# A two-block transformer kernel on one core: order of scores, exponentials and copies in its attention loops, and where the modulation matrix is multiplied

## The reference

```
first layer, differential attention (4 heads, two maps m = 0, 1 of width 64 each):
    p = softmax(q_m k_m^T / 8 - slope * |i - j|);  out = (p_0 - lam p_1) v
first layer, sparse attention (4 heads of width 64):
    of the allowed keys only the 256 with the highest index score count, the others get -inf
    out = softmax(q k^T / 8 - slope * |i - j|) v
second layer, forgetting attention (8 heads of width 64):
    cum_f = cumsum(log_sigmoid(f));  logits = q k^T / 8 + cum_f[q] - cum_f[k]  (causal)
second layer, modulation:
    mod = silu(c) @ w_ada + b_ada          (w_ada is 1024 x 6144, 24 MB)
```

## Time and profile before

| | |
|---|---|
| median of three runs | 3118.78 us |
| the profiled execution | 3110.41 us, span of its instructions 3108.7 us |
| TensorE busy | 2970.8 us, 96% |
| VectorE, ScalarE, GpSimd busy | 1343.3, 632.2, 1390.0 us |
| mean granted TensorE clock | 0.985 |
| loop of `diff` | about 434 to 559 us from the start |
| loop of `sparse` | about 559 to 655 us |
| loop of `forget` | about 1731 to 1886 us |

### The profile page before, as it was taken

The page is one execution under the profiler, slowest core; times in us unless marked ns, Lnnn a source line. Parts: engine busy times, 40 slices in busy tenths (PEclk is TensorE's granted clock), DMA queues, the critical chain, the costliest instruction groups (busy, mean ns, idle before and its releaser), DMA issues.

```text
span 3108.7 us, 33231 instructions
## 1 busy us (share of the span) xinstructions
PE 2970.8 (96%) x13501; PEld 2204.0 (71%) x13509; DVE 1343.3 (43%) x2012; ACT 632.2 (20%) x1056; POOL 1390.0 (45%) x814
## 2 busy tenths in 40 slices
PE   7999989889999999999999898999998999999997
PEld 4544446567888888888788556667667888887886
DVE  0499957646532324433514653111313433234323
ACT  1411036431110001111211462001112211111111
POOL 2000000035666566666677003444446666666663
PEclk8999999999999999999999999999999999999999
DMA  4111124532333333333433001332333233333331
GB/s 99 35 34 41 34 75 110 137 137 88 95 102 102 95 97 100 116 101 95 122 89 101 14 1 51 91 119 71 82 103 121 88 102 89 102 94 122 94 103 62
DMA packets 364919, 273.22 MB, mean 88 GB/s; under 512 B 14048, under 2 KB 334816, under 8 KB 364768
## 3 DMA queue, kind: packets, MB, share of 16 engines
q1 hardware_dynamic: 357568, 253.30, 28.4%
q10 hardware_dynamic: 4720, 10.68, 0.9%
q0 software_dynamic: 2480, 7.13, 0.7%
HBM read 262.59 MB, written 8.49 MB: 87 GB/s over the span
## 4 chain that ended last, share of the span: by engine, by line
PE 87%; DVE 4%; DMA 3%; issue 2%; POOL 2%; ACT 1%; SPq 0%; DVEq 0%; POOLq 0%; ACTq 0%
PE PS L809 39%; PE PS L821 24%; PE PS L761 5%; PE PS L775 4%; DMA ring<-in_w_in 3%; PE PS L446 2%; PE PS L1013 2%; PE PS L881 2%; PE PS L464 2%; PE PS L484 2%; POOL w_low L1883 1%; PE PS L476 1%; PE PS L895 1%; PE PS L738 1%; DVE arena L550 1%
## 5 line engine op out<-in xcount | busy, mean ns | idle before, releaser
L1883 POOL TENSOR_TENSOR w_low<-ring,w_high 128x1024 fp32r<-128x1024 f32 x382 | 938.1, 2456 | 31.8
L1880 POOL TENSOR_SCALAR w_high<-ring 128x1024 fp32r<-128x1024 f32 x382 | 425.7, 1114 | 1019.6 <-PE PS L821 371.6
L821 PE MATMUL PS<-w_high,hid_high 128*128 128x512 f32 x864 | 336.4, 389 | 9.1 <-issue 9.1
L821 PE MATMUL PS<-w_high,hid_low 128*128 128x512 f32 x864 | 336.2, 389 | 0.0
L821 PE MATMUL PS<-w_low,hid_high 128*128 128x512 f32 x864 | 336.1, 389 | 0.0
L809 PE MATMUL PS<-hT_high,w_high 128*128 128x512 f32 x656 | 271.6, 414 | 12.6 <-POOL w_low L1883 12.6
L809 PE MATMUL PS<-x1T_high,w_high 128*128 128x512 f32 x704 | 274.9, 390 | 3.6 <-DVE x1T_low L1574 3.6
L809 PE MATMUL PS<-x1T_low,w_high 128*128 128x512 f32 x704 | 274.6, 390 | 0.0
L809 PE MATMUL PS<-x1T_high,w_low 128*128 128x512 f32 x704 | 274.5, 390 | 0.0
L809 PE MATMUL PS<-hT_high,w_low 128*128 128x512 f32 x656 | 256.3, 391 | 0.0
L809 PE MATMUL PS<-hT_low,w_high 128*128 128x512 f32 x656 | 256.2, 391 | 0.0
(11 more groups left out here) (268 smaller groups left out, 4623.9 us busy)
## 6 DMA issues: line engine op xcount, KB each, us to landing
ring<-in_w_ff SPq DMA_DIRECT2D x128, 512.0 KB, 3.8
ring<-in_w_in SPq DMA_DIRECT2D x112, 512.0 KB, 3.9
ring<-in_w_gu SPq DMA_DIRECT2D x88, 512.0 KB, 3.9
ring<-in_w_ada SPq DMA_DIRECT2D x48, 512.0 KB, 5.2
ring<-in_w_down SPq DMA_DIRECT2D x44, 512.0 KB, 3.6
ring<-in_w_out SPq DMA_DIRECT2D x32, 512.0 KB, 4.2
ring<-in_w_branch SPq DMA_DIRECT2D x16, 512.0 KB, 3.9
arena<-in_x SPq DMA_DIRECT2D x8, 512.0 KB, 7.5
```

The costliest lines, as they stand in the source:

```text
L821: mm = pe.matmul(PS[:, 2 * p + half, :], x[:, k, at], w[:, q, half_of(half)], start=(first and n == 0), stop=(last and n == 2))
L1880: pool.tensor_scalar(w_high[:, q, :], ring[:, s, :], 1.0, 1.0, ALU.mult, ALU.mult).then_inc(weights_high, 1)
L1883: pool.tensor_tensor(w_low[:, q, :], ring[:, s, :], w_high[:, q, :].bitcast(F32), ALU.subtract).then_inc(weights_used[s], 1)
```

## The change

In a chunk of scores the added product of a map now follows that map's own scores: scores 0, added 0, scores 1, added 1. In ScalarE's step, `exps(u+1)` now stands before `copy_turned(u-1)`. Of the 12 groups of `ada`, `diff` now takes ten (two units in three, instead of six groups in two units of five) and `sparse` two (instead of six in every unit's fill). Before the loop of `forget`, `copy_v2(1)` now stands before the wait for `cum_done` and the copies to `cum_r`.

```diff
@@ scores(u), TensorE
-                        more = [None if self.more is None else self.more(pe, u, m, c, w) for m in range(2)]
                         for m in range(2):
                             if c == 0 and u >= 1:
                                 pe.wait_ge(self.logits_made, 2 * u - 1 + m)
+                            more = self.more(pe, u, m, c, w) if self.more is not None else None
                             mm = pe.matmul(PS[:, 2 * m + c // 512, 0:w], self.q(j, m, b), self.k(j, m, c, w),
-                                           start=True, stop=more[m] is None)
-                            if c + w == N and more[m] is None:
+                                           start=True, stop=more is None)
+                            if more is not None:
+                                mm = pe.matmul(PS[:, 2 * m + c // 512, 0:w], *more, start=False, stop=True)
+                            if c + w == N:
                                 mm.then_inc(self.scores_done, 1)
-                        for m in range(2):
-                            if more[m] is not None:
-                                mm = pe.matmul(PS[:, 2 * m + c // 512, 0:w], *more[m], start=False, stop=True)
-                                if c + w == N:
-                                    mm.then_inc(self.scores_done, 1)
@@ the loop of act(), ScalarE
                 for u in range(last + 2):
+                    if u < last:
+                        exps(u + 1)
                     if u >= 1:
                         copy_turned(u - 1)
-                    if u < last:
-                        exps(u + 1)
@@ ada_fill
-        def ada_fill(first, groups, every):
+        def ada_fill(first, groups):
             def fill(pe, u):
-                if u % every < 2 and u // every < groups:
+                if u % 3 < 2 and u // 3 < groups:
                     for j in range(2):
-                        ada(pe, 4 * (first + u // every) + 2 * (u % every) + j)
+                        ada(pe, 4 * (first + u // 3) + 2 * (u % 3) + j)
             def after(act, u):
-                if u % every == 1 and u // every < groups:
-                    rows_out(act, first + u // every)
+                if u % 3 == 1 and u // 3 < groups:
+                    rows_out(act, first + u // 3)
-        fill_c, rows_c = ada_fill(6, 6, 2)
+        fill_c, rows_c = ada_fill(10, 2)
@@ diff
-            prob, probT, (4, 5), *ada_fill(0, 6, 5))
+            prob, probT, (4, 5), *ada_fill(0, 10))
@@ ScalarE before forget.act
             for u in range(1, 4):
                 copy_tiles("qk2", 1, u, qk2T)
+            copy_v2(1)
             act.wait_ge(cum_done, 1)
             for r in (slice(0, 8), slice(64, 72)):
                 act.copy(cum_r[r, :], fl[0:8, :]).then_inc(cum_high, 1)
-            copy_v2(1)
             forget.act(act)
```

## The result

The changed kernel takes 3198.90 us (median of four runs, 3195.68 to 3201.08), the kernel before on the same chip 3118.66 us. The ratio is 1.0263, with a 95% interval of 1.0244 to 1.0282: 80 us slower. The forecast was 3182 us with a range of 3150 to 3212.

A forecast was written before the change was run, and what follows sets the result against it. TensorE, busy 96% of the span, was taken to bound the kernel. `diff` 12, `sparse` 9 and `forget` 21.9 + 20 made 62.9 us on 3110.4: 3173.3, or 3182 at the median's level, range 3150 to 3212.

The forecast's parts named there:

- Part 1: Before `forget`: copies to `cum_r` behind `copy_v2` delay VectorE's whole queue and the first logits, +21.9 us.
- Part 2 in `forget`: ScalarE's copies, now behind the exponentials, make TensorE wait: 5.25 us a pass, taken as +20 us.
- The four places: In a `forget` pass, block 7 next +1.9, block 7 turned +1.0, block 5 next +0.6, block 5 turned +1.75 us.
- Part 2 in `diff`: Late copies delay `times_v`: 3.1 us a pass, 12.4 in four, of which 5 us kept because fills cover waits.
- Part 3: Added product between the maps' scores: 0 in `forget`, where maps still overlap; 15.7 us in `sparse`, where they run serially.
- Part 4: Fills of four `ada` groups move: +7.7 us in `diff`, -7.7 in `sparse`, which also loses three waits, -3.8.
- the nearly free part 2: Rival: early exponentials free VectorE and TensorE, and `sparse` idle time hides longer scores; 3148 us, chance 0.08.
- strict order: Rival: TensorE keeps matmuls in program order, so `forget` loses its map overlap too, +30 us; 3212 us, chance 0.13.
- the other side: Rival: exponentials in front end the three loops' idle time, up to -47.8 us against +21.9; 3093 us, chance 0.03.

The follow-up runs named there:

- part 1 alone: Kernel before with only `copy_v2(1)` moved ahead of the wait for `cum_done` and the copies to `cum_r`: 3135.50 us, ratio 1.0057.
- part 2 alone: Kernel before with only `exps(u+1)` put before `copy_turned(u-1)` in all three loops: 3160.46 us, ratio 1.0138.
- The added work: Whole change plus 16 unread float32 products in each of the twelve `sparse` units left without a fill: 3189.15 us, ratio 1.0233 against the kernel before.
- part 3 alone: Kernel before with only each map's added product put right behind its own scores: 3124.58 us, ratio 1.0020.
- any single part: Kernel before with one edit: `copy_v2` first 3135.50 us, exponentials first 3160.46, added product behind its scores 3124.58, `ada` groups ten and two 3108.23.
- pairs: Kernel before with two edits: score order and `ada` groups 3120.01 us; exponentials first and score order 3181.58; exponentials first and `ada` groups 3151.87.

## Why the prediction was right, and where its sum was off

The direction, the range and the order of size were right: 63 us forecast, 80 measured. Point by point:

- **Part 1, forecast +21.9, measured +18.** The mechanism is as described, instruction by instruction. The step "between 1711.25 and 1734.76 it has no hole that could take up a delay" was true and not enough: the stretch was stretched by GpSimd beside it, and 4 us of that vanished when it moved. The step "TensorE, with one unit of scores done" was wrong, since that unit waited as well (5.8 us with part 1 alone), but it changes nothing in the sum: the logits come last.
- **Part 2 in `forget`, forecast +20, measured +30.6.** The four places were real. With part 2 alone, in the pass of the earlier trace rows, the four together move TensorE by about 5 us where I had 5.25. The last three of them:

```profile
1815.60 1.06 PE L464 MATMUL PS<-ident,arena 128*128 128x128 f32 x8 [1.28 <-ACT arena L524]
1827.49 0.87 PE L484 MATMUL PS<-arena 128*64 128x256 f32 x8 [0.55 <-ACT arena L524]
1834.73 0.84 PE L464 MATMUL PS<-ident,arena 128*128 128x128 f32 x6 [2.18 <-ACT arena L524]
```

  In the earlier trace rows the same instructions waited 0.33, 0 and 0.55 us. After block 7 the change waits 1.69 us for the copies before `times_v`, where I had 1.9:

```profile
1844.09 3.18 PE L481 MATMUL PS<-arena 128*64 128x256 f32 x16 [1.69 <-ACT arena L521]
```

  That row also shows what the sum had left out: the same 16 instructions took 1.73 us before and 3.18 here, straight after the wait. The waits, 16.7 us more, are the term as forecast, a little smaller; the rest goes with 35 us more of low clock, which the sum had put at nothing.
- **Part 2 in `diff`.** Forecast 12.4 uncovered and 5 with the fills. Measured 13.4 alone, and 8.9 - 2.7 = 6.2 on top of the fills. Both numbers are near, and part of that is luck. The sum took only the new waits for copies, which grew by 11.7 us; 5.7 us of other waits went, so TensorE idled 5.9 us more, and lower clock made up the rest. Most of what the fills save is that clock, and 2 us of it are waits.
- **Part 3, forecast 0 in `forget` and 15.7 in `sparse`, measured 0 and 10.4.** The halves of the rows run side by side. In `sparse` they don't. Two of its chunks in a unit of block 7 after the change:

```profile
630.28 1.12 PE L446 MATMUL PS<-arena 64*128 64x512 f32 x2
631.65 1.12 PE L446 MATMUL PS<-arena 64*128 64x512 f32 x2 [0.25 <-issue]
632.71 0.39 PE L449 MATMUL PS<-arena 128*128 128x512 bf16 x1
633.03 1.12 PE L446 MATMUL PS<-arena 64*128 64x512 f32 x2
```

  Map 1 starts 1.37 us after map 0. From chunk to chunk it is 633.03 - 630.28 = 2.75 us, against 1.60 before:

```profile
608.47 1.13 PE L446 MATMUL PS<-arena 64*128 64x512 f32 x4
609.76 0.38 PE L452 MATMUL PS<-arena 128*128 128x512 bf16 x1 [0.16 <-issue]
610.07 1.13 PE L446 MATMUL PS<-arena 64*128 64x512 f32 x4
```

  So a chunk of 512 costs 1.15 us more, and the 1.13 was right. The idle time of 0.16 us before the mask, here and in the earlier trace rows, is none. The kernel has two mask products there, and the next chunk's row shows both (611.13, x2); in this one the profile holds only the second. In the rows after, the mask behind the first map is missing in the same way. A map's scores take 1.05 us from their start to the mask's, and the next scores start 0.32 us after the mask's, where one mask follows another in 0.23. That the loop paid 5 us less than forecast goes with 3.5 us less of idle time (15.9 to 12.4 us) and with a clock of 0.99 instead of 0.97.
- **Part 4, forecast +7.7 in `diff` and -11.5 in `sparse`, measured +2.7 and -9.2.** Right in `sparse`. In `diff` the sum charged every fill in full and took off nothing for the 10.9 us of idle time that the earlier trace rows showed; 3 us of that took up fills.
- **The interaction in `sparse`, forecast none, measured 23 us.** This is the step that was mis-sized. The sentence on the clock in part 1 ("it falls there in this place already") treated it as a matter of one place. The loop has 49 us at the lower level, 43 more than before, and at half speed that can cost up to 43 / 2 = 21 us. The added work took away the low clock and 15 of the 23.

Two statements beside the sum were wrong. TensorE does have holes outside the loops: of its 138 us of idle time, 90 lie there. The conclusion drawn from it held, since the stretch between the loops kept its length. And the time of 3148 for the nearly free part 2 left out the 11.5 us that part 4 takes off `sparse`; it would have been 3137.

Of the rivals, strict order fell with part 3 alone, and the nearly free part 2 and the other side fell with part 2 alone. That the range held the time owes something to chance: its upper end came from the rival of strict order, which was false, and the time there came from the clock.

## What to carry to other kernels

For an engine with an in-order queue, look at what stands behind two neighbours before you swap them. In this kernel the swap on ScalarE alone cost 43 us: copies that gate TensorE must not stand behind work that waits for TensorE. And an edit that spreads waits over a TensorE loop can cost more than its waits, since the clock can fall and make the remaining work slower. Read the granted clock of the loop's window, and treat filler work as possibly worth more than its place. Interactions of this kind don't show in edits tested one at a time. Before you read a loop's clock from one execution, see how much it differs between kernels that run the same loop.

## What the runs showed of the hardware beyond that

- In `sparse`, the granted clock stood between 0.95 and 0.99 with any single part, at 0.95, 0.90 and 0.89 with pairs, and at 0.81 with all four, though TensorE was modelled busy for 109 of 129 us there. It fell four times. Within 1.8 us before each fall the engine had ended a hole of 1.78, 1.55, 3.59 or 3.21 us, a wait for ScalarE's copies; after a hole of 1.75 us that ended at 639.40 it did not fall. At the lower level a chunk of 512 columns of one map took 2.55 us from start to start, against 1.37 at full clock:

```profile
650.28 2.07 PE L446 MATMUL PS<-arena 64*128 64x512 f32 x2
652.83 2.07 PE L446 MATMUL PS<-arena 64*128 64x512 f32 x2 [0.47 <-issue]
654.83 0.61 PE L449 MATMUL PS<-arena 128*128 128x512 bf16 x1
```

- In `forget` with part 3, matmuls on one half of TensorE's rows are not held up by an earlier one on the other half: the scores of the two maps start 0.01 us apart (1802.84) and take 1.13 us together, while map 0's added product, which stands between them in program order, starts at 1803.40.
- VectorE instructions of 0.17 us each took 4.50 us for four beside GpSimd's weight splits, 0.78 us without them. The first of the four took 0.91 us and the third 3.14; the first ended 0.03 us after the shorter split, the third 0.03 us after the memset that follows the longer one. The Trainium skill, "SBUF — State Buffer", section "SBUF: two separate sides", describes a port pair that GpSimd and VectorE, in some of its modes, lock against each other for a whole instruction; the trace agrees, in that the two slow instructions end with GpSimd's. In which mode VectorE ran them no row shows.
